# Root and shift of the RMS norms taken out of the activations and put behind the products

## What is computed

```python
sh1, sc1, gt1, sh2, sc2, gt2, sh3, sc3, gt3 = modulation(cond, ada_w[l], ada_b[l])
h = rms_norm(x, norm_g[l, 0]) * (1 + sc1) + sh1
x = x + 0.5 * gt1 * swiglu(h, ffn_w1[l, 0], ffn_w2[l, 0])
h = rms_norm(x, norm_g[l, 1]) * (1 + sc2) + sh2
p = h @ w_in[l]                      # retention and RWKV in layer 0, mLSTM and attention in layer 1
x = x + gt2 * (mixers(p) @ w_out[l])
h = rms_norm(x, norm_g[l, 2]) * (1 + sc3) + sh3
x = x + 0.5 * gt3 * swiglu(h, ffn_w1[l, 1], ffn_w2[l, 1])
```

## Time and profile before

| | |
|---|---|
| median of 3 runs | 3367.52 us (3366.03 to 3369.59) |
| the profiled execution, its time and its span | 3385.92 us, 3384.2 us |
| PE busy | 3083.6 us, 91% |
| DVE, ACT, POOL busy | 44%, 29%, 7% |
| mean granted clock of TensorE | 0.941 of full speed |

### The profile page before, as it was taken

The page is one execution under the profiler, slowest core; times in us unless marked ns, Lnnn a source line. Parts: engine busy times, 40 slices in busy tenths (PEclk is TensorE's granted clock), DMA queues, the critical chain, the costliest instruction groups (busy, mean ns, idle before and its releaser), DMA issues.

```text
span 3384.2 us, 60102 instructions
## 1 busy us (share of the span) xinstructions
PE 3083.6 (91%) x25821; PEld 2908.3 (86%) x25821; DVE 1474.9 (44%) x2009; ACT 982.8 (29%) x1361; POOL 237.6 (7%) x313
## 2 busy tenths in 40 slices
PE   6999998879688789999999999989886798899998
PEld 4999997769478678999988999989786568899997
DVE  3655653325365446656646322232343443322232
ACT  3321213222433224312214312222354353331221
POOL 0000000000465000000000000000010000000000
PEclk8999999969699899999999999999788799999999
DMA  5443432011000022434433222212001002121221
GB/s 212 146 153 124 145 130 76 26 44 44 2 10 4 2 100 100 153 128 143 152 111 108 98 86 75 85 47 69 7 13 44 4 1 88 50 85 65 75 89 41
DMA packets 68068, 265.14 MB, mean 78 GB/s; under 512 B 7776, under 2 KB 7904, under 8 KB 67456
## 3 DMA queue, kind: packets, MB, share of 16 engines
q1 hardware_dynamic: 47808, 184.72, 16.0%
q0 software_dynamic: 20032, 76.98, 6.8%
HBM read 257.87 MB, written 3.81 MB: 77 GB/s over the span
## 4 chain that ended last, share of the span: by engine, by line
PE 87%; DVE 6%; ACT 4%; issue 1%; DMA 1%; POOL 0%; SPq 0%; DVEq 0%; ACTq 0%; POOLq 0%
PE ps L1860 35%; PE ps L1861 34%; PE ps L1719 1%; PE ps L1950 1%; PE ps L1951 1%; PE ps L1699 1%; PE ps L1405 1%; PE ps L907 1%; PE ps L1707 1%; PE ps L891 1%; PE ps L897 1%; DMA ring<-w_ada 1%; PE ps L547 1%; PE ps L939 1%; PE ps L959 1%
## 5 line engine op out<-in xcount | busy, mean ns | idle before, releaser
L336 DVE TENSOR_TENSOR w_lo<-ring,w_hi 128x1024 fp32r<-128x1024 f32 (+1 forms) x307 | 401.5, 1308 | 1239.0 <-ACT w_hi L331 1237.8
L331 ACT ACTIVATE w_hi<-ring 128x1024 fp32r<-128x1024 f32 (+1 forms) x307 | 345.5, 1126 | 1470.8 <-PE ps L1861 1254.1
L1860 PE MATMUL ps<-h_hi,w_hi 128*128 128x320 f32 x1944 | 613.4, 316 | 98.7 <-DVE w_lo L336 52.6
L1861 PE MATMUL ps<-h_hi,w_hi 128*128 128x320 f32 x1944 | 604.6, 311 | 0.0
L1860 PE MATMUL ps<-h_lo,w_hi 128*128 128x320 f32 x1944 | 604.5, 311 | 0.0
L1861 PE MATMUL ps<-h_lo,w_hi 128*128 128x320 f32 x1944 | 604.4, 311 | 0.0
L1860 PE MATMUL ps<-h_hi,w_lo 128*128 128x320 f32 x1944 | 604.2, 311 | 0.0
L1861 PE MATMUL ps<-h_hi,w_lo 128*128 128x320 f32 x1944 | 603.9, 311 | 0.0
L1860 PEld LDWEIGHTS ps<-h_hi,w_hi 128*128 128x128 f32 x1944 | 368.0, 189 | 117.9 <-issue 87.8
L1861 PEld LDWEIGHTS ps<-h_hi,w_hi 128*128 128x128 f32 x1944 | 368.9, 190 | 0.0
L1860 PEld LDWEIGHTS ps<-h_lo,w_hi 128*128 128x128 f32 x1944 | 368.5, 190 | 0.0
(11 more groups left out here) (349 smaller groups left out, 3995.0 us busy)
## 6 DMA issues: line engine op xcount, KB each, us to landing
late_mem<-w_ada POOLq DMA_DIRECT2D x128, 512.0 KB, 3.6
ring<-w_up0a SPq DMA_DIRECT2D x44, 512.0 KB, 3.3
ring<-w_up0b SPq DMA_DIRECT2D x44, 512.0 KB, 3.3
ring<-w_up1a SPq DMA_DIRECT2D x44, 512.0 KB, 3.3
ring<-w_up1b SPq DMA_DIRECT2D x44, 512.0 KB, 3.2
ring<-w_down0a SPq DMA_DIRECT2D x16, 704.0 KB, 4.1
ring<-w_down0b SPq DMA_DIRECT2D x16, 704.0 KB, 4.0
ring<-w_down1a SPq DMA_DIRECT2D x16, 704.0 KB, 4.0
```

The costliest lines, as they stand in the source:

```text
L331: act.activation(w_hi[:, n % SPLITS, 0:cols], ring[:, r, 0:cols], ACT.Copy).then_inc(high_ready, 1)
L336: dve.tensor_tensor(w_lo[:, n % SPLITS, 0:cols], ring[:, r, 0:cols], w_hi[:, n % SPLITS, 0:cols].bitcast(F32), ALU.subtract).then_inc(spli ...
L1860: pe.matmul(left, weights, acts[:, k, LEFT], start=start, stop=stop)
L1861: mm = pe.matmul(right, weights, acts[:, k, RIGHT], start=start, stop=stop)
```

## The change

For the products behind the five inner norms, `h_hi` and `h_lo` are now the two parts of `x * gs` alone (`gs` is norm weight times 1 + scale); no root, no shift. They can be made as soon as a block of `x` is done, and are made inside the loop of the down or out stage that makes `x`: ACT rounds (`prepare`), DVE subtracts (`gained_low`). The shift vectors (prompt and sample) stand as two more columns ahead of the 640 tokens, so the left matmul of each block has 322 columns, and each tile yields the products of the two shifts beside those of the tokens. Where the tile is read, DVE copies the two columns to `shifts`, multiplies the tile by `rs` into SBUF (`rooted_tile`), and the shift product is added there: by the bias of ACT's Silu or Identity, now in two parts (prompt, sample), or by DVE's `scalar_tensor_tensor` for the odd up tiles.

The sum of squares changes too: ACT squares each block in the same loop, POOL adds the eight one after another, and PE takes a single block through the matrix of ones. PE does this after tile 0 of the next product; ACT reads the sum from PSUM with Ln (scale and bias inside). norm0 of layer 0 keeps root and shift in the activations, with the sum after both groups of the modulation.

Moved besides: `out` reads its operands from `mix_hi` and `mix_lo` instead of `h_hi` and `h_lo`; 56 instead of 60 modulation rows are taken in the second FFN of layer 0 and 16 instead of 12 in the next; layer 0's groups 3 to 7 are finished before `down0b` and group 8 after; PE, ACT and DVE wait for the late tables after the projection instead of before it; SP's queue is not changed, and POOL's queue gets the sums between its streams of row loads.

```diff
-                        pe.matmul(left, weights, acts[:, k, LEFT], start=start, stop=stop)
-                        mm = pe.matmul(right, weights, acts[:, k, RIGHT], start=start, stop=stop)
+                        pe.matmul(left, weights, acts[:, k, at_left], start=start, stop=stop)
+                        mm = pe.matmul(right, weights, acts[:, k, at_right], start=start, stop=stop)
...
                             if k == k_blocks - 1:
                                 mm.then_inc(tiles_done, 1)
+                                if root is not None:
+                                    norm(layer, root)
...
-                pairs_read(layer, name)
-                for k in range(DB):
-                    pe.wait_ge(sq_ready, norms[0] * DB + k + 1)
-                    pe.wait_ge(loaded, 32)
-                    pe.matmul(left, C("ones"), squares(name)[:, k, LEFT], start=(k == 0), stop=(k == DB - 1))
-                    mm = pe.matmul(right, C("ones"), squares(name)[:, k, RIGHT], start=(k == 0), stop=(k == DB - 1))
+                pe.wait_ge(free_dve, free0[layer, name] + 1 - SETS)
+                pe.wait_ge(loaded, 32)
+                pe.wait_ge(sq_added, SUMS * (q + 1))
+                pe.matmul(left, C("ones"), square(q, 0)[:, LEFT], start=True, stop=True)
+                mm = pe.matmul(right, C("ones"), square(q, 0)[:, RIGHT], start=True, stop=True)
...
+                def prepare(k):
+
+                    act.wait_ge(x_ready, x0[layer, name] + k + 1)
+                    if q < len(NORMS) - 1:
+                        j = int(step[-1])
+                        if k == 0:
+                            act.activation(h_hi[:, :, 0:EDGE], mod[after][:, 3 * j * DB:(3 * j + 1) * DB, :], ACT.Copy)
+                        act.activation(h_hi[:, k, H_PROMPT], x[:, k, PROMPT], ACT.Copy, scale=gs[:, j, k, 0:1])
+                        act.activation(h_hi[:, k, H_SAMPLE], x[:, k, SAMPLE], ACT.Copy, scale=gs[:, j, k, 1:2])\
+                           .then_inc(h_high, 1)
+                    if k > 2:
+                        act.wait_ge(sq_added, SUMS * q + k - 2)
+                    act.activation(square(q, k), x[:, k, :], ACT.Square).then_inc(sq_ready, 1)
...
+            def root(layer, name):
+
+                act.wait_ge(norm_ready, norms[0] + 1)
+                turn(act.activation(rs[:, :], pair(blk0[layer, name] % SETS)[2], ACT.Ln, scale=1.0 / D_MODEL,
+                                    bias=C("eps")))
+                act.sem_inc(free_dve, 1)
+                act.activation(rs[:, :], rs[:, :], ACT.Exp, scale=-0.5).then_inc(root_ready, 1)
...
-                    act.activation(dst[:, i * 4 + u, :], pair((b0 + u) % SETS)[2], ACT.Copy)\
-                       .then_inc(proj_ready, 1)
+                    act.wait_ge(late_ready, i * 4 + l0 + u + 1)
+                    act.activation(dst[:, i * 4 + u, PROMPT], dst[:, i * 4 + u, PROMPT], ACT.Identity,
+                                   bias=shifts[:, u, 0:1])
+                    act.activation(dst[:, i * 4 + u, SAMPLE], dst[:, i * 4 + u, SAMPLE], ACT.Identity,
+                                   bias=shifts[:, u, 1:2]).then_inc(proj_ready, 1)
...
+            def rooted_tile(layer, name, i, u, b0, to):
+
+                dve.wait_ge(root_ready, norms[0] + 1)
+                dve.tensor_copy(shifts[:, u, :], edge((b0 + u) % SETS))
+                dve.tensor_tensor(to, pair((b0 + u) % SETS)[2], rs[:, :], ALU.mult).then_inc(late_ready, 1)
...
+            def norm(q):
+
+                for k in range(1, DB):
+                    pool.wait_ge(sq_ready, DB * q + k + 1)
+                    if k > 1:
+                        pool.wait_ge(sq_added, SUMS * q + k - 1)
+                    pool.tensor_tensor(square(q, 0), square(q, 0), square(q, k), ALU.add).then_inc(sq_added, 1)
```

More of the change, by code:

```diff
@@ L368, in build, with square, after_norm @@
         mix = mx.take(DB, NT)
-        def squares(name):
-            return mix if name == "norm2" else y
+        NORMS = [(0, "norm0"), (0, "norm1"), (0, "norm2"), (1, "norm0"), (1, "norm1"), (1, "norm2"), (DEPTH, "norm")]
+        BEFORE = {1: (0, "down0b"), 2: (0, "out"), 3: (0, "down1b"), 4: (1, "down0b"), 5: (1, "out"), 6: (1, "down1b")}
+        SUMS = DB - 1
+        def square(q, k):
+            if q == 0:
+                return y[:, k, :]
+            return normed[:, 1, :] if k == 0 else prod[:, k % 2, :]
+        def after_norm(layer, name):
+            return name in PROJECTIONS or name[:2] == "up" and (layer, name[2]) != (0, "0")
+        late0, lates = {}, 0
+        for layer in range(DEPTH):
+            for name, blocks, k in stages(layer):
+                late0[layer, name] = lates
+                lates += blocks if after_norm(layer, name) else 0
         STEPS = {"up0a": 0, "down0a": 22, "up0b": 30, "down0b": 52}
         STEPS.update({f"{name[:-2]}1{name[-1]}": at for name, at in list(STEPS.items())})
-        MD_FIRST = {(0, 0): (0, 56), (0, 1): (56, 60), (1, 0): (116, 12)}
+        MD_FIRST = {(0, 0): (0, 56), (0, 1): (56, 56), (1, 0): (112, 16)}
         MD_LATE = (N_MOD - EARLY) * DB
         MD_ALL = MD_LATE + N_MOD * DB
-        MOD_READY = {(0, 0): 2, (0, 1): 4, (0, 2): 4, (1, 0): 5, (1, 1): 5, (1, 2): 6}
+        MOD_READY = {(0, 0): 2, (0, 1): 4, (0, 2): 4, (1, 0): 6, (1, 1): 6, (1, 2): 7}
         def md_tile(layer, name, t):
@@ L1854, in block @@
                     left, right, _ = pair((b0 + u) % SETS)
+                    if late:
+                        left = wide((b0 + u) % SETS)
                     s = (n0 + u) % SPLITS
@@ L1959, in _ @@
                 for j in range(3):
-                    if layer or j:
-                        norm(layer, f"norm{j}")
-                    if j == 1:
-                        pe.wait_ge(loaded, 16 * (4 + layer))
-                    ready = (h_ready, DB * (norms[0] - 1))
+                    first = layer == j == 0
+                    root = None if first else f"norm{j}"
+                    ready = (h_ready, DB * (norms[0] - first))
                     if j != 1:
@@ L1972, in _ @@
                     elif layer == 0:
-                        linear(layer, "ret", RET_BLOCKS, DB, h_hi, h_lo, ready=ready)
+                        linear(layer, "ret", RET_BLOCKS, DB, h_hi, h_lo, ready=ready, root=root)
+                        pe.wait_ge(loaded, 16 * 4)
                         tensor_retention(pe)
@@ L1982, in _ @@
                     if j == 1:
-                        linear(layer, "out", DB, DB, h_hi, h_lo, ready=(mix_split, DB * layer))
+                        linear(layer, "out", DB, DB, mix_hi, mix_lo, ready=(mix_split, DB * layer))
             norm(DEPTH, "norm")
@@ new lines, in first_norm @@
+            def first_norm():
+                for k in range(DB):
+                    act.activation(y[:, k, :], x[:, k, :], ACT.Square).then_inc(sq_ready, 1)
+                ada(0)
+                root(0, "norm0")
+                act.wait_ge(mod_ready, MOD_READY[0, 0])
+                for k in range(DB):
+                    act.wait_ge(scaled, k + 1)
+                    act.activation(h_hi[:, k, H_PROMPT], normed[:, k % 2, PROMPT], ACT.Identity,
+                                   bias=mod[0][:, k, 0:1])
+                    act.activation(h_hi[:, k, H_SAMPLE], normed[:, k % 2, SAMPLE], ACT.Identity,
+                                   bias=mod[0][:, k, 1:2]).then_inc(h_high, 1)
@@ L2101, in _ @@
                     for k in range(DB):
-                        act.activation(h_hi[:, k, :], mix[:, k, :], ACT.Copy).then_inc(mix_high, 1)
-                    only_parts(layer, "out", DB)
-            norm(DEPTH, "norm", None)
+                        act.activation(mix_hi[:, k, :], mix[:, k, :], ACT.Copy).then_inc(mix_high, 1)
+                    only_parts(layer, "out", DB, norms[0])
+            root(DEPTH, "norm")
         @block.vector
@@ L2243, in one @@
                     f = u // 2
+                    if late:
+                        rooted_tile(layer, name, i, u, b0, (prod if u % 2 else silu)[:, f % 2, :])
                     if u % 2:
@@ L2303, in _ @@
                         free_tiles(0, DB)
-                    norm(layer, f"norm{j}", j, modulation if (layer, j) == (0, 0) else None)
+                        first_norm()
                     if j != 1:
```

284 lines of the change are left out of this document (169 added, 115 removed).

## The result

The changed kernel takes 3269.3 us (median of 4 runs, 3266.5 to 3270.3), the one before 3367.0 beside it. The ratio is 0.9707, with a 95% interval from 0.969 to 0.9724: 97.8 us faster. I had forecast 3239 and a range from 3225 to 3260. The sign was right, the size 30 us too good, and the time fell outside the range.

A forecast was written before the change was run, and what follows sets the result against it. PE, 91% busy, bounds the kernel, so only its gaps at norms pay. -130.8 + 5.4 - 7 - 5 + 4.0 + 5.2 = -128.2 us, from 3367.5 to 3239.3; range 3225 to 3260 for 8 in 10.

The forecast's parts named there:

- I take the same difference off it: Base of the forecast time: the median lies 16.7 us below the profiled span, and the same was taken off 3256.
- Two more columns: Left matmuls of 183 tiles, 24 each: two columns at 0.9 ns in proportion add 4 us, or nothing.
- rival A: Rows of 642 make the moved operand read slower over 8784 matmuls: 10% slower cancels the gain, 20% gives 3496; chance 0.06.
- Inner norms: PE's gaps at the five norms inside the layers: 130.8 us removed, 5.4 us added for fp32 sums.
- Covers: After each inner norm's last tile, ready PE work hides splits and sums; 1.1 us spare at tile 1, 2.6 at tile 3.
- Rival B: Small stalls stay at each norm as covers fail: 2 to 5 us each, 3249 to 3264 in all; chance 0.2.
- norm0: Layer 0's first norm: sums come last, group 1 ends some 10 us sooner; gain 7 us, bounds 3 and 10.
- Final norm: From last residual to first output, 13.8 us before, 8.2 to 9.2 after: gain 5 us.
- Projection tails: End of a projection, where nothing covers: 2.0 us against 0.7 before the mixer, 1.3 more four times, 5.2 us.
- Rivals C and D: C: DVE binds in up stages with modulation rows or `rwkv`, 3309, chance 0.05; D: weight ring comes due, 3303, chance 0.03.
- T + 7.7: At an inner norm, POOL's last add of squares ends 7.7 us after T, when the last tile is seen as done.

The follow-up runs named there:

- the moved rows alone: Kernel before with only `h_hi` and `h_lo` in rows of 642, two unused columns ahead of the tokens: 3400.8 us, ratio 1.0094.
- the fillers: 19 needless fp32 matmuls of 256 columns put into PE's waits in retention: changed kernel with them 3251.6 us, kernel before with them 3363.0 us.

## Why the forecast missed

- **"I take the same difference off it" failed, and was the largest part: about 21 of the 30 us.** The distance of 16.7 us between the profiled span and the median before is no property of profiling. The kernel before falls into one of two cases in each execution, about half and half (40 of 74 in the lower one), with 19 us between them, which in the one profile of the lower case are retention's clock. Its profile was of the upper case, its three runs of the lower. The changed kernel's profile was of the upper case, and nine of its ten times, 3264 to 3273, lie about that execution's 3266.5. So an equal sum lands at 3256 + 1.7 (an execution's time is 1.7 above its span), not at 3239: 18.4 of the 21. The other 2.7 are that the changed kernel's profiled execution was itself below its median. The numbers to see it by were in front of me: three runs from 3366 to 3370, and one profiled execution at 3385.9, 18.4 off the median or five times their spread.
- **"Two more columns" was mis-sized: 4 us forecast, about 16 measured.** 183 late tiles x 0.073 = 13.4, and 44 tiles of layer 0's first FFN, whose operands have the new offset but no columns, at 7.316 instead of 7.256 us, 2.6. By these two numbers the columns themselves are the small part: 183 x 0.013 = 2.4 us, under the 4 forecast. The other 13.6, 0.060 in each of 227 tiles, come with the moved rows, which I had put at nothing outside rival A, and whose 8784 matmuls leave those 44 tiles out. I bounded the term by proportion (0.022 per tile) from above and by nothing from below, and gave dearer cases to rival A with a threshold of 10%. Between 0.3% and 10% I had put nothing.
- **Inner norms: right.** Without the slower tiles (175 of the 183 lie in these stages, x 0.073 = 12.8; the first FFN's 2.5), it is -109.2 - 12.8 - 2.5 = -124.5 against -130.8 + 5.4 = -125.4. The method, pricing a gap by the delay of a later tile, held to 1%.
- **Covers: right**, with 1.1 us of margin as forecast for the first (split done at 534.06, PE's first matmul of tile 1 at 535.14) and 1.7 instead of 2.6 for tile 3. Rival B did not come: PE is busy for all 27 us of the window at norm1.
- **norm0: 4.8 of 7**, within the bounds of 3 and 10. What failed is that group 1 would come 10 us sooner. It came 6.2 sooner, and then waited for its weights.
- **Final norm: 4.8 of 5**, right.
- **Projection tails: right in step, hidden in the sum.** Ahead of the mixer PE now idles for 2.18 us where it idled for 0.79, 1.39 against 1.3 forecast:

```profile
620.38 3.23 PE L540 MATMUL ps<-rest,cst 128*128 128x512 f32 x4 [2.18 <-ACT rest L2145]
```
```profile
645.98 0.70 PE L499 MATMUL ps<-rest,cst 128*128 128x512 f32 x1 [0.79 <-ACT rest L2068]
```

  (first the changed kernel, then the one before). In the sum it drowns: mLSTM became 7.3 us shorter, RWKV 3.9 and attention 3.1 longer. mLSTM's mean granted clock is 0.83 against 0.82, attention's 0.85 against 0.87; attention's loss was there with the moved rows alone, and what moves the other two was not pinned down.
- **Rivals C and D: no sign.** Where DVE has the modulation rows beside the new work, 19 tiles of `up1b` in layer 0 took 138.74 us after 137.37, and 11 of `rwkv` 78.18 after 77.38: 0.07 more per tile, as everywhere. ACT's roundings in the rows above still wait for PE, not for a DMA.
- **The range** was built from bounds inside the sum. The base from which the sum is taken had none. With a 19 us case on it, the range would have reached 3260 + 19 = 3279.

Not settled: what decides, execution by execution, which case an unfilled kernel takes. The runs show only that with the fillers ahead the short case came each time. Nor is it known why the changed kernel, whose retention is the same code, took the upper case in both its profiles; one of its ten times, 3256, may have been the lower.

## What to carry to other kernels

Before a forecast is taken off a median, see that the profiled execution is one of the crowd: where it stands far from runs that agree among themselves, find the stretch that differs, or put the distance into the range. Where PE works in short bursts behind a wait, look at the granted clock of what follows; needless matmuls in the wait can be worth more than the wait (17.4 us against 8.3 here). And a term that multiplies by every tile deserves an upper bound from something worse than proportion: 1% of a tile was 16 us here.

## What the hardware showed

- **A moved operand's start.** With float32r rows of 642, each 8 bytes further off, a matmul of 320 columns came 148.2 ns after the last instead of 146.7 (7.113 and 7.040 us over 48), and 146.2 with rows of 656. Two more columns on every second matmul cost 0.013 us per tile on rows of 642 and 0.04 on aligned ones, and 14 more 0.12.
- **Granted clock.** The same instructions of retention (from the first score to the last output) ran 39 us at about half clock or 22.5 us at full clock, in executions of one program; 14 fillers in the wait ahead, and 5 more in the bursts, gave full clock in both that were profiled, and one level of times in the 12 runs of the kernel before.
- **POOL and DVE beside each other.** An add of 128x640 took 1.53 us with DVE idle (at 3248.39) and 2.37 beside work with two SBUF inputs. At the add of 487.68 DVE's `h_lo` took 2.33 us for two, where it takes 1.01 alone; at norm1 a DVE product of 16 columns took 1.54 us and ended with POOL's add (537.90 + 1.54 = 539.44, 537.64 + 1.76 = 539.40), where another of this size took 0.17:

```profile
487.68 2.37 POOL L2461 TENSOR_TENSOR normed<-normed,prod 128x640 f32<-128x640 f32 x1 [5.98 <-ACT prod L2063]
...
488.53 2.33 DVE L2300 SCALAR_TENSOR_TENSOR h_lo<-x,gs,h_hi 128x128 fp32r<-128x128 f32 x2
...
537.90 1.54 DVE L2254 TENSOR_TENSOR mod<-mod,par 128x16 f32<-128x16 f32 x1
```

  The Trainium skill, SBUF — State Buffer, section SBUF: two separate sides, has one port pair for the two engines, and one of them blocked while the other holds it. These rows agree: each of the two lasted up to 1.4 us longer beside the other here, all of it under cover, and the add that counted still ended at T + 7.7.
